# The heads of the first block: a projection in two halves of twelve matmuls instead of four quarters of six

## What is computed

```python
for l in range(DEPTH):                       # DEPTH = 2
    u = rms_norm(h, attn_norm[l])
    proj = einsum('bsd,dc->bsc', u, w_in[l]) # 1024 -> 7424 columns
    dq, dk, dv, rq, rk, rv, rg, gq, gk, gv, gate_logits = split_cols(proj, IN_SPLITS)
    ...
    a = differential_attention(dq, dk, dv, lam)       # 4 heads, two maps each
    r = bidirectional_retention(rq, rk, rv, ...)      # 4 heads, with decay
    r = silu(rg) * head_group_norm(r, ret_group_norm[l])
    c = grouped_query_attention(gq, gk, gv)           # 8 query heads, 2 key heads
    merged = sum(sigmoid(gate_logits) * einsum(branches, w_branch[l]))
    h = h + merged @ w_out[l]
    ...                                               # MLP
```

## Time and profile before

| | us |
|---|---|
| median of three runs | 3919.05 |
| lowest, highest | 3911.23, 3919.33 |
| the profiled execution | 3911.92 |
| its span, first to last instruction | 3910.1 |
| TensorE busy in it | 3700.8 |
| VectorE, ScalarE busy | 1639.3, 1435.0 |

### The profile page before, as it was taken

One profiled execution on the slowest core, in us unless ns is written; L12 is line 12 of the kernel. 1 busy time (PEld: TensorE's weight loads), 2 busy tenths in 40 slices (PEclk: granted clock), 3 DMA queues, 4 the chain that ended last, 5 costly groups with the idle time before them and its releaser, 6 DMA issues.

```text
span 3910.1 us, 45566 instructions
## 1 busy us (share of the span) xinstructions
PE 3700.8 (95%) x17055; PEld 2666.8 (68%) x17055; DVE 1639.3 (42%) x2308; ACT 1435.0 (37%) x2172; POOL 2.4 (0%) x9
## 2 busy tenths in 40 slices
PE   6998999999999999999999799889999989989998
PEld 4555787777755557867777654378888865357886
DVE  5564434333356653343332544342222244534333
ACT  5554323333345542233333343423322334433333
POOL 0000000000000000000000000000000000000000
PEclk8999999999999999999999899999999999999999
DMA  3111233555521112335555110012222221012332
GB/s 100 44 49 44 76 92 102 140 147 143 144 54 44 44 49 82 96 103 145 150 144 160 36 43 1 0 44 64 64 64 59 64 73 49 0 40 82 94 92 79
DMA packets 570338, 303.17 MB, mean 78 GB/s; under 512 B 26017, under 2 KB 564977, under 8 KB 570225
## 3 DMA queue, kind: packets, MB, share of 16 engines
q1 hardware_dynamic: 568496, 299.32, 27.0%
q10 hardware_dynamic: 1728, 2.36, 0.2%
HBM read 299.55 MB, written 2.10 MB: 77 GB/s over the span
## 4 chain that ended last, share of the span: by engine, by line
PE 88%; DVE 7%; ACT 3%; issue 2%; DMA 0%; SPq 0%; DVEq 0%; ACTq 0%
PE ps L963 13%; PE ps L965 12%; PE ps L964 12%; PE ps L1149 10%; PE ps L1151 10%; PE ps L1153 10%; PE ps L1320 2%; PE ps L1303 2%; PE ps L1280 2%; PE ps L1056 1%; PE ps L1087 1%; PE ps L1000 1%; PE ps L1068 1%; PE ps L1258 1%; DVE vst L2132 1%
## 5 line engine op out<-in xcount | busy, mean ns | idle before, releaser
L1418 ACT ACTIVATE whi<-wraw 128x1024 fp32r<-128x1024 f32 x448 | 471.0, 1051 | 576.7 <-DMA wraw<-in_w_mlp 252.9
L963 PE MATMUL ps<-uhi,whi 128*128 128x512 f32 x1440 | 628.0, 436 | 19.0 <-DVE ulo L1891 19.0
L1874 DVE TENSOR_TENSOR wlo<-wraw,whi 128x1024 fp32r<-128x1024 f32 x448 | 547.1, 1222 | 133.8 <-ACT whi L1418 124.1
L964 PE MATMUL ps<-ulo,whi 128*128 128x512 f32 x1440 | 571.5, 397 | 0.0
L965 PE MATMUL ps<-uhi,wlo 128*128 128x512 f32 x1440 | 571.4, 397 | 0.0
L963 PEld LDWEIGHTS ps<-uhi,whi 128*128 128x128 f32 x1440 | 271.7, 189 | 159.1 <-issue 90.5
L1149 PE MATMUL ps<-u2hi,whi 128*128 128x512 f32 (+1 forms) x1024 | 315.4, 364 | 34.3 <-DVE u2lo L2125 32.1
L964 PEld LDWEIGHTS ps<-ulo,whi 128*128 128x128 f32 x1440 | 272.9, 189 | 74.5 <-issue 22.1
L965 PEld LDWEIGHTS ps<-uhi,wlo 128*128 128x128 f32 x1440 | 271.9, 189 | 66.2
L1151 PE MATMUL ps<-u2lo,whi 128*128 128x512 f32 (+1 forms) x1024 | 309.5, 358 | 0.0
L1153 PE MATMUL ps<-u2hi,wlo 128*128 128x512 f32 (+1 forms) x1024 | 308.8, 357 | 0.0
(11 more groups left out here) (250 smaller groups left out, 4576.2 us busy)
## 6 DMA issues: line engine op xcount, KB each, us to landing
wraw<-in_w_in SPq DMA_DIRECT2D x128, 512.0 KB, 3.7
wraw<-in_w_mlp SPq DMA_DIRECT2D x128, 512.0 KB, 4.0
mod_raw<-in_w_mod SPq DMA_DIRECT2D x96, 512.0 KB, 5.3
wraw<-in_w_mlp_in SPq DMA_DIRECT2D x64, 512.0 KB, 4.3
wraw<-in_w_mlp_out SPq DMA_DIRECT2D x64, 512.0 KB, 4.0
wraw<-in_w_branch SPq DMA_DIRECT2D x16, 512.0 KB, 3.4
wraw<-in_w_out SPq DMA_DIRECT2D x16, 512.0 KB, 3.9
wraw<-in_w_o SPq DMA_DIRECT2D x16, 512.0 KB, 3.9
```

Source lines behind the costliest of these rows:

```text
L963: pe.matmul(bank, whs[:, i], x_hi[:, k], start=(i == 0), stop=False)
L964: pe.matmul(bank, whs[:, i], x_lo[:, k], start=False, stop=False)
L1418: act.activation(whi[:, r], wraw[:, r], ACT.Copy).then_inc(w_hi, 1)
L1874: dve.tensor_tensor(wlo[:, r], wraw[:, r], whi[:, r].bitcast(F32), ALU.subtract).then_inc(w_split, 1)
```

## The change

A projection is put down as two steps instead of four: a "part" at its first quarter and the step "project" at its third. TensorE emits twelve matmuls at each. The due times of all other steps stay as they are, as does the length of a projection in them. So a step due in the second or fourth quarter keeps its place against the projection's matmuls. One due in the first or third quarter has six more of them in front of it, and one due in the third quarter now stands behind the whole projection and its eviction. The gates' products and the second block are not touched.

```diff
 PARTS = 4
+HALVES = 2
...
     def project(use, columns, **more):
         at = PARTS * len(ends)
         whole = Step("project", use=use, columns=columns, layer=layer, **more)
-        for i in range(PARTS - 1):
-            put(at + i, "part", index=i, head=whole)
-        events.append((at + PARTS - 1, len(events), whole))
+        put(at, "part", index=0, head=whole)
+        events.append((at + PARTS // HALVES, len(events), whole))
...
-                        whole, i = (step.head, step.index) if step.name == "part" else (step, PARTS - 1)
+                        whole, i = (step.head, step.index) if step.name == "part" else (step, HALVES - 1)
...
-                                             range(KT * i // PARTS, KT * (i + 1) // PARTS),
+                                             range(KT * i // HALVES, KT * (i + 1) // HALVES),
```

## The result

| | before | after |
|---|---|---|
| median, us | 3919.19 (4 runs, 3911.23 to 3920.88) | 3983.77 (4 runs, 3982.39 to 3984.42) |
| span of the profiled execution | 3910.1 | 3981.4 |
| TensorE busy | 3700.8 | 3722.5 |

What follows compares the result with a forecast made beforehand. TensorE, busy 95% of the span, was taken as the bound. Per layer 21.2 + 3.7 + 3.4 + 4.1 - 7.7 = 24.7 us, 49 over two, plus 4 of clock on 3911.9 gave 3965, range 3936 to 3990.

Steps and rivals of the forecast that it cites:

- New waits behind an eviction: TensorE waits for steps now queued behind a projection's eviction on ScalarE: 21.2 us a layer, one swish attend included.
- swish steps: Attend of diff 3 behind the swish eviction, +1.8 us; gqa 3.1 behind the swish product on VectorE, +3.7, per layer.
- diff 0.3: Differential unit whose turn follows the projection's end at once, its exponentials behind the eviction: wait 5.2 us instead of 1.00.
- Less cover alone: Gqa 0.1, diff 1.3 and diff 3.2 lose six matmuls of cover with unchanged queues: +3.4 us a layer.
- four steps priced at 4.1 together: Retention score 1.2, retention's attend 1.6, a final sum 0.9, a second turn 0.4: each loses the quarter behind its producer.
- What gets shorter: Old waits at steps that gain six matmuls of cover, such as gqa 2.2 and retention scores: -7.7 us a layer.
- TensorE's own work: TensorE's matmuls and small steps in the mixed stage: unchanged, 0 us.
- 33 vanished borders: Places per layer where a small step no longer follows a projection piece: 0 us, at most 6 in all.
- The clock: TensorE's lower clock after long waits, drawn by one wait of four: +4 us.
- Every long wait draws the lower clock: Rival: twelve long waits at 1.8 us each slow TensorE's clock, 3981 us, up to 4000; chance 0.18.
- Most is hidden: Rival: each new wait only replaces the next, as VectorE and ScalarE have idle time, 3912 us; chance 0.08.
- Faster: larger cover: Rival: ScalarE evicts earlier in its existing pauses, only the shorter waits remain, 3891 us; chance 0.07.

Runs made afterwards that it cites:

- e1_queue: The changed kernel with eviction and swish product back at the fourth quarter, TensorE still in halves: 1.0028 of the kernel before, median 3926.4 us.
- e2_swish: The changed kernel with only the swish projections evicted at the fourth quarter again: 1.0204 of the kernel before, median 3991.7 us.
- e3_shift: The changed kernel with halves at the second and fourth quarter and the eviction back at the fourth: 1.015 of the kernel before, median 3971.5 us.
- e7_fill: The changed kernel plus 112 unread matmuls a layer in front of twelve waiting steps: 1.0115 of the kernel before, median 3958.3 us.

## Why the prediction held, step by step

The forecast was 3965 within 3936 to 3990, and 3984 came. From profiled execution to profiled execution it foretold 53 us and 71.3 came: 51.1 of waits for 49, 23.5 of clock for 4, and -3.3 in the rest for nothing. So the account of the waits was right in the main, that of the clock much too small, and the range held the result because its upper end had been set to take in a rival.

**New waits behind an eviction: right in kind and step by step.** Foretold were 24.7 us a layer, after all gains and losses. The sum over layer 0 went from 25.0 to 50.5, so 25.5. That the sum is so close is in part luck: the swish steps were 2.2 too high and the gains 1.7 too low, against 1.6 too little for lost cover and 2.3 of waits that nobody had foreseen. The steps behind an eviction by themselves are no luck. Single steps in layer 0, as growth of the wait, forecast and measured: diff 0.3 4.1 and 4.2; diff 2.2 2.6 and 2.5; diff 1.2 1.4 and 1.6; diff 3.1 1.0 and 1.1; attend 0 2.5 and 2.6; gqa 1.2's second turn 2.5 and 2.7; gqa 0.2's 1.0 and 1.2; attend of gqa 2 0.9 and 0.8; the retention score at gqa 2.1 with its next turn 3.4 and 3.6.

**The swish steps: too high, by 1.2 and 1.0.** Attend of diff 3 got 0.6 instead of 1.8, and gqa 3.1 2.7 instead of 3.7. ScalarE and VectorE there, against the earlier trace rows:

```profile
362.56 1.28 ACT L1435 ACT_TABLE_LOAD   x1
363.85 0.60 ACT L1435 ACTIVATE gateb<-ps 128x512 f32<-128x512 f32 x1
```

```profile
364.55 0.69 DVE L1939 TENSOR_TENSOR gateb<-gateb,ps 128x512 f32<-128x512 f32 x1 [0.72 <-ACT gateb L1435]
365.15 0.68 DVE L1891 TENSOR_TENSOR blo<-fo,bhi 128x512 fp32r<-128x512 f32 x1
```

And the end of the projection and the turn on TensorE:

```profile
363.08 0.39 PE L965 MATMUL ps<-uhi,wlo 128*128 128x512 f32 x1
366.69 0.66 PE L1068 MATMUL ps<-ident,probs 128*128 128x128 f32 x4 [3.22 <-DVE probs L2008]
```

E is 363.47, but the table load started at 362.56, 0.9 ahead of it: the load waits for no result, only the sigmoid behind it does. I had let the load begin at E, because in the earlier trace rows it began behind a *decay_exp* that ended about there. So the product started 1.08 after E and not 1.93. And the product is only half of the cause of the growth: e1_queue and e2_swish show 1.93 us of this wait without it, from six matmuls of lost cover, which the prediction gave to gqa 0.1, diff 1.3 and diff 3.2 but not to this unit. The load takes 1.28 us and the activation starts 1.29 after the load's start, so no further drain shows, as in the kernel before.

**Less cover alone: 3.4 foretold, 4.8 came** (gqa 0.1 +1.0, diff 1.3 +2.1, diff 3.2 +1.6). Of the four steps priced at 4.1 together, the four largest growths that I can place in that group (retention's attend 1.6, retention score 0.2 1.4, a turn of gqa 3.3 0.8, the final sum 0.6) make 4.3. Three waits grew that stand nowhere in the prediction: turns of diff 0.2 and diff 2.1 by 0.8 each and one of gqa 3.2 by 0.7. e3_shift shows this way by itself, and at a larger size.

**What gets shorter: 7.7 foretold, 9.4 came.** That is 1.5 at gqa 2.2, 1.2 at the second turn of gqa 3.1, 1.5, 1.4 and 1.3 at the retention scores, 0.9 in two small ones; and 1.6 at gqa 1.1, an old wait that I had not seen going.

**TensorE's own work: right, with the clock apart.** The number of matmuls is the same, and with the waits filled (e7_fill) the stages less waits and less filler are 730.0, beside 731.6 before. By this difference the 33 vanished borders a layer gave some 1.6 us of the 6 that I kept for the low end. But the sign that I had announced, a busy time within 5 us, failed: it rose by 21.7, since matmuls at the lower clock are busy longer (0.63 us instead of 0.40 in the rows above). Two of the smaller signs missed too: turns behind L2004 came to 21.5 us a layer and not about 17, *attend* to 3.4 and not about 5.

**The clock: the term that was mis-sized.** I took "one of four" from four old waits of 2.2 to 2.8 us, of which one showed the lower clock, and put it at +4. It is +23.5, in 16 spells instead of one; what came is the rival "Every long wait draws the lower clock", with its 3981. Its price was near too: it had 1.8 for each of twelve waits, and 23.5 over 16 spells is 1.5. Two things failed. The waits were miscounted: over 2.2 us there are eight a layer and not six. And a share found at waits of 2.2 to 2.8 was carried to waits of up to 5.2: each of the 16 spells stands at or behind a wait of 2.1 us or more, and the two stages have 20 of these, so four in five drew one and not one in four. The length of the wait does not settle it, for the same wait of 2.60 at diff 0.2 drew one in layer 1 and none in layer 0. The page "TensorE: Matmul & The Clock Gate" of the Trainium skill, section "What's actually happening", which has the clock follow how busy TensorE has been of late, speaks for this rival, and the traces now agree with it: the clock of 0.83 behind the wait of 5.23, and 1.00 in the same place when it is filled.

**The other rivals.** "Most is hidden" fell at attend 0 and diff 0.3, where the waits came whole. "Faster: larger cover" fell at the same places, for the reason that it named itself: no cover stands behind those evictions.

## What to carry to other kernels

Where one list sets the order on all engines, a step that is moved on the busiest engine moves in the queues of the others too. Ask first which steps are then queued behind an operation that must wait, and give the two places due times of their own: that alone brought back 65 of 75 us in the stages here, and moving the eviction half a quarter the other way beat the kernel before by 0.3%. When a change makes waits of several microseconds on TensorE, count about half as much again for the slow matmuls behind them: here 51 us of new waits brought another 23.5. The half is this kernel's figure.

## What the chip showed that I had not expected

TensorE's lower clock comes readily inside dense work. In stages where TensorE was busy for 374 of 425 us, matmuls behind waits started 0.43 us apart instead of 0.23, and the two stages were at the lower level for 61.4 us in 16 spells. Matmuls of no use in front of the longest waits left one spell of 3.4 us, and made the kernel 25 us faster than without them.

The rest of the program, the same code in all twelve kernels, took between 3122 and 3136 us in their profiled executions (3128.5 before, 3125.2 after). The clock record goes with most of it: the waits there are within 2.6 us of each other, while the time at the lower level goes from 141 to 176 us, and the longest rest, of e1_queue, has the most. So differences of a few microseconds between two of these kernels are better read from the stages, and there from the waits first, than from the whole time.
